# First mixer of a two-block network: parameters in two transfers, x in eight, the norm's sums by token on TensorE, and fewer small VectorE operations

## The reference

```
h = rmsnorm(x, even_norm)                  # over 1024 features of each token
p = h @ even_w_in                          # 2048 columns: u (512), z (1024), pool (512)
u -> state-space layer (32 groups of 16 channels, complex decay exp(dt * (a_re + i a_im)),
     dt = exp(log_dt)), evaluated in chunks of 8 tokens: a Toeplitz part inside
     a chunk and a scan over 64 chunks
pool -> four causal running means (windows 2, 4, 8, 16), minus the input, times pool_w and pool_scale
out = (concat(pool, glu(s5)) * silu(z)) @ even_w_out ; x = x + out
```

## Time and profile before

| what | us |
|---|---|
| median of 3 runs | 2919.9 (2909.63 to 2922.06) |
| the profiled execution, its own time | 2919.66 |
| its span, first to last instruction | 2917.9 |
| TensorE busy in the span | 2700.2 (93%) |
| VectorE busy | 1556.8 (53%) |
| ScalarE busy | 948.7 (33%) |
| GpSimd busy | 351.6 (12%) |

### The profile page before, as it was taken

One profiled execution on the slowest core, in us unless ns is written; L12 is line 12 of the kernel. 1 busy time (PEld: TensorE's weight loads), 2 busy tenths in 40 slices (PEclk: granted clock), 3 DMA queues, 4 the chain that ended last, 5 costly groups with the idle time before them and its releaser, 6 DMA issues.

```text
span 2917.9 us, 31891 instructions
## 1 busy us (share of the span) xinstructions
PE 2700.2 (93%) x13104; PEld 2103.4 (72%) x13104; DVE 1556.8 (53%) x2110; ACT 948.7 (33%) x1536; POOL 351.6 (12%) x303
## 2 busy tenths in 40 slices
PE   4889997899999988799999999999999977999997
PEld 3667665678888766486788888888878634788885
DVE  8975897654433478645533334433365457443332
ACT  2214321532222442552323223222232435332321
POOL 1001000122210000010222102221000000122200
PEclk9889999899999998799999999999999879999998
DMA  3252211122232221001322332232323200132232
GB/s 113 78 92 94 89 44 50 66 88 101 94 101 91 79 69 58 22 2 37 102 99 96 96 100 94 94 101 90 98 90 107 67 15 1 58 101 95 98 100 69
DMA packets 75810, 229.02 MB, mean 78 GB/s; under 512 B 16656, under 2 KB 17936, under 8 KB 75280
## 3 DMA queue, kind: packets, MB, share of 16 engines
q1 hardware_dynamic: 62880, 213.51, 22.2%
q0 software_dynamic: 1840, 5.77, 1.0%
q10 hardware_dynamic: 10944, 7.70, 0.9%
HBM read 221.18 MB, written 5.77 MB: 78 GB/s over the span
## 4 chain that ended last, share of the span: by engine, by line
PE 72%; DVE 19%; ACT 4%; issue 2%; DMA 1%; ACTq 1%; POOL 0%; DVEq 0%; SPq 0%; POOLq 0%
PE ps L353 71%; DVE mem L370 6%; DVE mem L383 5%; DVE part L440 3%; ACT part L428 1%; PE ps L364 1%; DMA mem<-lag_dram 1%; DVE mem L548 1%; DVE mem L2793 1%; DVE ps L370 1%; ACT mem L504 1%; DMA mem<-in_w_even 1%; ACTq L1100 1%; DVE mem L376 0%; DVE mem L388 0%
## 5 line engine op out<-in xcount | busy, mean ns | idle before, releaser
L353 PE MATMUL ps<-part,part 128*128 128x512 f32 (+1 forms) x9624 | 2212.8, 391 | 71.4 <-DVE part L523 27.3
L353 PEld LDWEIGHTS ps<-part,part 128*128 128x128 f32 x9624 | 1799.4, 190 | 482.8 <-issue 45.7
L440 DVE TENSOR_TENSOR part<-mem,part 128x1024 fp32r<-128x1024 f32 (+2 forms) x421 | 560.1, 1337 | 588.3 <-ACT part L428 587.8
L428 ACT ACTIVATE part<-mem 128x1024 fp32r<-128x1024 f32 (+2 forms) x421 | 418.5, 1003 | 234.9 <-DMA mem<-in_ffb_down 56.4
L370 DVE TENSOR_TENSOR mem<-ps,mem 128x512 f32<-128x512 f32 (+3 forms) x356 | 221.8, 623 | 351.1 <-PE ps L353 336.6
L353 PE MATMUL ps<-mem 128*64 128x64 f32 (+14 forms) x2728 | 341.6, 333 | 60.5 <-DVE mem L370 29.6
L353 PEld LDWEIGHTS ps<-mem 128*64 128x64 f32 (+4 forms) x2728 | 214.8, 170 | 173.8 <-issue 88.8
L512 POOL TENSOR_TENSOR mem<-mem 128x512 f32<-128x512 f32 x70 | 92.5, 1321 | 1378.7 <-ACT mem L504 1376.9
L370 DVE TENSOR_TENSOR mem<-mem 128x512 f32<-128x512 f32 (+13 forms) x335 | 169.7, 506 | 41.5 <-ACT mem L1490 11.4
L1463 ACT ACTIVATE part<-mem 128x512 fp32r<-128x512 f32 x88 | 55.6, 632 | 328.6 <-DVE mem L370 328.6
L1472 POOL TENSOR_TENSOR mem<-mem 128x512 f32<-128x512 f32 x88 | 113.9, 1294 | 378.8 <-ACT mem L1460 378.8
(11 more groups left out here) (160 smaller groups left out, 907.5 us busy)
## 6 DMA issues: line engine op xcount, KB each, us to landing
mem<-in_ffa_gate SPq DMA_DIRECT2D x44, 512.0 KB, 3.2
mem<-in_ffa_up SPq DMA_DIRECT2D x44, 512.0 KB, 3.2
mem<-in_ffb_gate SPq DMA_DIRECT2D x44, 512.0 KB, 3.2
mem<-in_ffb_up SPq DMA_DIRECT2D x44, 512.0 KB, 3.2
mem<-in_ffa_down SPq DMA_DIRECT2D x32, 512.0 KB, 3.5
mem<-in_ffb_down SPq DMA_DIRECT2D x32, 512.0 KB, 3.6
mem<-in_w_odd SPq DMA_DIRECT2D x24, 512.0 KB, 3.2
mem<-in_w_ab SPq DMA_DIRECT2D x22, 512.0 KB, 3.2
```

The lines of the kernel that those rows point to most:

```text
L353: return e.matmul(out, l, r, start=start, stop=stop, skip_group_check=True)
L428: w.e.activation(K.wts[c % NH].h[:, 0:n], K.raws[c % NR][:, 0:n], ACT.Copy).then_inc(*K_A.up(("w", c)))
L440: w.e.tensor_tensor(t.l, K.raws[c % NR][:, 0:n], t.hf, SUB).then_inc(*K.V.up(("w", c)))
```

## The change

The columns that VectorE needs first (`even_norm`, `log_dt`, `a_re`, `a_im`, 104 of the 816) come by a transfer of their own, `params0`. The other 712 are issued later by ScalarE, behind its last square, and `ssm_bc` behind them. SP issues weight chunk 0 first, then x in eight transfers of one tile. VectorE and ScalarE start with `params0` alone. GpSimd no longer adds the squares: TensorE multiplies each 128x128 piece of each square tile by a column of ones, so that the sums of a token come out with tokens as rows (128x4 in place of 128x512), and the scale, reciprocal and root run on 128x4. To get the factor back along the row, VectorE multiplies the identity by the four columns (`spread`, 128x512), TensorE multiplies that by ones, and ScalarE copies the result out of PSUM into `rstd`. `exp_small` has 15 operations in place of 22, `even_u_vector` one of 512 columns in place of eight of 64 (the chunk is now reversed when it is read back from DRAM), and the pool takes its mean and difference in one operation.

The diff, without the lists of semaphore names and of host arrays:

```diff
@@ -26,7 +26,7 @@
 
 
 COLS = [
-    ("even_norm", 8), ("pool_scale", 4), ("ssm_d", 8), ("log_dt", 32), ("a_re", 32), ("a_im", 32),
+    ("even_norm", 8), ("log_dt", 32), ("a_re", 32), ("a_im", 32), ("pool_scale", 4), ("ssm_d", 8),
     ("odd_norm", 8), ("conv_w", 248), ("conv_b", 8), ("ln_g", 8), ("ln_b", 8), ("final_norm", 8),
     ("ffa_norm", 16), ("mix_norm", 16), ("ffb_norm", 16), ("mu", 14), ("w0", 4), ("a0", 4),
     ("kk", 4), ("ka", 4), ("rk", 4), ("lnw", 4), ("lnb", 4), ("subln", 1), ("mconv_w", 16),
@@ -37,6 +37,7 @@
 for _name, _n in COLS:
     COL[_name] = NCOL
     NCOL += _n
+FIRST = COL["pool_scale"]
 
 
 CONSTS = [
@@ -675,6 +676,7 @@
         self.ys = bc.rearrange("p (q i c) -> p q i c", q=4, i=LC)
         high = m.tiles(5)
         self.y = [late[:, 2048 + T * i:2048 + T * i + T] for i in range(3)] + [high[:, i, :] for i in range(5)]
+        self.root, self.spread = K.rT, K.nb[2]
         self.lags = K.nb01.rearrange("p (a n) -> p a n", a=8)
 
     def part(self, a, tl):
@@ -691,9 +693,18 @@
     E, e = K.even, w.e
     K.ring(0, 1, 2, 3, 4, 5, 6, 7)
     h_ready = lambda k: (K.V, ("h", 0, k))
+    sums = K.take(w, ("msT", 0), K.V)
+    for k in range(8):
+        w.wait_ge(*K.A["sq", 0, k])
+        for t in range(NT):
+            done = mm(e, sums[:, t:t + 1], K.sq[k % 2][:, t * P:(t + 1) * P], K.cc("ones", 0, 1), k == 0 and t == 0,
+                      k == 7)
+        done.then_inc(*K.P.up(("summed", k), *([("msT", 0)] if k == 7 else [])))
     for o in linear(K, w, "even_u", 4, 8, K.h, h_ready, K.V):
         if o == 0:
-            norm_tensor(K, w, 0, K.ss)
+            acc = K.take(w, "even_factor", K.A)
+            w.wait_ge(*K.V["even_spread"])
+            mm(e, acc, K.cc("ones"), E.spread, True, True).then_inc(*K.P.up("even_factor"))
     zed = linear(K, w, "even_z", 8, 8, K.h, h_ready, K.V)
     pool = linear(K, w, "even_pool", 4, 8, K.h, h_ready, K.V)
     next(zed)
@@ -771,19 +782,17 @@
 def exp_small(w, E, out, in_, *names):
 
     t0, t1, t2 = E.v[6:9]
-    ts(w, t0, in_, 1.0 / math.log(2.0), None, MUL, None)
-    ts(w, t0, t0, -126.0, 126.0, MAX, MIN)
-    ts(w, t0, t0, 12582912.0, None, ADD, None)
+    ts(w, t0, in_, 1.0 / math.log(2.0), -126.0, MUL, MAX)
+    ts(w, t0, t0, 126.0, 12582912.0, MIN, ADD)
     ts(w, t0, t0, -12582912.0, None, ADD, None)
     stt(w, t1, t0, -0.693359375, in_, MUL, ADD)
     stt(w, t1, t0, 2.12194440e-4, t1, MUL, ADD)
     ts(w, t1, t1, -0.7, 0.7, MAX, MIN)
-    ts(w, t2, t1, 1.0 / 5040, 1.0 / 720, MUL, ADD)
-    for c in (1.0 / 120, 1.0 / 24, 1.0 / 6, 0.5, 1.0, 1.0):
-        tt(w, t2, t2, t1, MUL)
-        ts(w, t2, t2, c, None, ADD, None)
+    ts(w, t2, t1, 1.0 / 5040, None, MUL, None)
+    for c in (1.0 / 720, 1.0 / 120, 1.0 / 24, 1.0 / 6, 0.5, 1.0):
+        stt(w, t2, t2, c, t1, ADD, MUL)
     ts(w, E.v[12].bitcast(I32), t0, 127.0, 8388608.0, ADD, MUL)
-    tt(w, out, t2, E.v[12], MUL, *names)
+    stt(w, out, t2, 1.0, E.v[12], ADD, MUL, *names)
 
 
 def even_angles(K, w):
@@ -927,8 +936,7 @@
     E = K.even
     w.wait_ge(*K.P["even_u", o])
     acc, factor = positions(K.acc("even_u", o)), positions(K.rstd)
-    for d in range(LC):
-        tt(w, E.us[:, o, 64 * d:64 * d + 64], acc[:, 7 - d, :], factor[:, 7 - d, :], MUL, ("even_u", o))
+    tt(w, E.us[:, o, :].rearrange("p (j c) -> p j c", j=LC), acc, factor, MUL, ("even_u", o))
 
 
 def even_z_vector(K, w, o):
@@ -957,8 +965,8 @@
         sh *= 2
     oth = a[0] if cur is not a[0] else a[1]
     tt(w, oth[:, 0:16], cur[:, 0:16], K.cc("invpos", 16 * o, 16), MUL)
-    ts(w, oth[:, 16:T], cur[:, 16:T], 1.0 / width, None, MUL, None)
-    tt(w, E.pooled[o % 2], oth, u, SUB, ("pooled", o))
+    stt(w, E.pooled[o % 2][:, 16:T], cur[:, 16:T], 1.0 / width, u[:, 16:T], MUL, SUB)
+    tt(w, E.pooled[o % 2][:, 0:16], oth[:, 0:16], u[:, 0:16], SUB, ("pooled", o))
     weights_lo(K, w, K.first[0] + 12 + o + 4)
 
 
@@ -968,13 +976,19 @@
     even_angles(K, w)
     weights_lo(K, w, c + 1)
     for k in range(8):
-        w.wait_ge(*K.landed(f"x{k // 2}"))
+        w.wait_ge(*K.landed(f"x{k}"))
         gained_vector(K, w, 0, k, lambda k: K.pc("even_norm", k))
+    weights_lo(K, w, c + 2)
+    w.wait_ge(*K.landed("consts"))
+    w.wait_ge(*K.landed("params"))
+    rstd_vector(K, w, ("msT", 0), E.root, K.acc("msT", 0)[:, 0:4], 1.0 / 1024, 1e-6)
     weights_lo(K, w, c + 3)
+    w.wait_ge(*K.A["rstd", ("msT", 0)])
+    tt(w, E.spread.rearrange("p (t n) -> p t n", t=NT), b(K.cc("ident"), [P, NT, P], 1), b(E.root, [P, NT, P], 2), MUL,
+       "even_spread")
     even_factors(K, w)
-    rstd_vector(K, w, ("ms", 0), K.rstd, K.acc("ms", 0), 1.0 / 1024, 1e-6)
     even_powers(K, w)
-    w.wait_ge(*K.A["rstd", ("ms", 0)])
+    w.wait_ge(*K.A["even_factor"])
     even_u_vector(K, w, 0)
     weights_lo(K, w, c + 4)
     even_u_vector(K, w, 1)
@@ -1050,19 +1064,25 @@
 def even_scalar(K, w):
     E, e = K.even, w.e
     c = K.first[0]
-    e.dma_start(E.bc, K.io["ssm_bc"]).then_inc(*K.counts["ssm_bc"].up("landed", by=16))
     weights_hi(K, w, c + 1)
     for k in range(8):
-        w.wait_ge(*K.landed(f"x{k // 2}"))
+        w.wait_ge(*K.landed(f"x{k}"))
         gained_scalar(K, w, 0, k, lambda k: K.pc("even_norm", k))
-        square_scalar(K, w, 0, k, K.ss, K.sq)
+        if k > 1:
+            w.wait_ge(*K.P["summed", k - 2])
+        e.activation(K.sq[k % 2], K.x[:, k, :], ACT.Square).then_inc(*K.A.up(("sq", 0, k)))
+    e.dma_start(K.prm[:, FIRST:NCOL], K.io["params"]).then_inc(*K.counts["params"].up("landed", by=16))
+    e.dma_start(E.bc, K.io["ssm_bc"]).then_inc(*K.counts["ssm_bc"].up("landed", by=16))
+    weights_hi(K, w, c + 2)
+    rstd_scalar(K, w, ("msT", 0), E.root)
     weights_hi(K, w, c + 3)
     w.wait_ge(*K.V["angle"])
     e.activation(E.turn, E.angle, ACT.Abs).then_inc(*K.A.up("turn"))
     e.activation(E.si, E.angle, ACT.Sin).then_inc(*K.A.up("sine"))
+    w.wait_ge(*K.P["even_factor"])
+    e.activation(K.rstd, K.acc("even_factor"), ACT.Copy).then_inc(*K.A.up("even_factor"))
     w.wait_ge(*K.V["quarter"])
     e.activation(E.co, E.turn, ACT.Sin).then_inc(*K.A.up("cosine"))
-    rstd_scalar(K, w, ("ms", 0), K.rstd)
     for o in range(4):
         weights_hi(K, w, c + o + 4)
     for o in range(8):
@@ -1078,7 +1098,7 @@
                 w.wait_ge(*K.landed(f"u_out{tl}"))
                 for d in range(LC):
                     e.dma_start(E.u[16 * d:16 * d + 16, 8 * tl:8 * tl + 8, :],
-                                K.u_dram[tl].rearrange("(g h) d c -> d h g c", h=16)[d]).then_inc(
+                                K.u_dram[tl].rearrange("(g h) j c -> j h g c", h=16)[7 - d]).then_inc(
                         *K.counts[f"u_in{tl}"].up("landed", by=16))
         if o == 4:
             for i in range(2):
@@ -1130,9 +1150,7 @@
 def even_gpsimd(K, w):
     E, e = K.even, w.e
     c = K.first[0]
-    for k in range(8):
-        square_gpsimd(K, w, 0, k, K.ss, K.sq)
-    w.wait_ge(*K.P["ms", 0])
+    w.wait_ge(*K.P["even_factor"])
     zeros = K.nb[2]
     memset(w, zeros, 0.0)
     w.wait_ge(*K.G.now)
@@ -3027,9 +3045,6 @@
 def sync(K, e):
 
     w = Waits(e, K.P)
-    for i in range(4):
-        e.dma_start(K.x[:, 2 * i:2 * i + 2, :], K.io["x"][:, 2 * i:2 * i + 2, :]).then_inc(
-            *K.counts[f"x{i}"].up("landed", by=16))
     for c, (src, n, _) in enumerate(K.weights):
         if c >= NR:
             w.wait_ge(*K.lo_count(c - NR)["w", c - NR])
@@ -3037,6 +3052,9 @@
         if len(src.shape) == 3:
             dst = dst.rearrange("p (a b) -> p a b", a=src.shape[1])
         e.dma_start(dst, src).then_inc(*K.counts[f"raw{c % NR}"].up(c, by=16))
+        if c == 0:
+            for k in range(8):
+                e.dma_start(K.x[:, k, :], K.io["x"][:, k, :]).then_inc(*K.counts[f"x{k}"].up("landed", by=16))
     w.wait_ge(*K.V["final", 9, 7])
     e.dma_start(K.io["out"], K.x).then_inc(*K.counts["out"].up("landed", by=16))
     w.wait_ge(*K.landed("out"))
@@ -3045,7 +3063,6 @@
 def tensor(K, e):
     w = Waits(e, K.P)
     w.wait_ge(*K.landed("consts"))
-    w.wait_ge(*K.landed("params"))
     even_tensor(K, w)
     odd_tensor(K, w)
     swiglu_tensor(K, w, 3)
@@ -3060,8 +3077,7 @@
 
 def vector(K, e):
     w = Waits(e, K.V)
-    w.wait_ge(*K.landed("consts"))
-    w.wait_ge(*K.landed("params"))
+    w.wait_ge(*K.landed("params0"))
     even_vector(K, w)
     odd_vector(K, w)
     swiglu_vector(K, w, 3, 4, lambda k: K.pc("mix_norm", k))
@@ -3076,9 +3092,9 @@
 
 def scalar(K, e):
     w = Waits(e, K.A)
-    e.dma_start(K.prm[:, :], K.io["params"]).then_inc(*K.counts["params"].up("landed", by=16))
+    e.dma_start(K.prm[:, 0:FIRST], K.io["params0"]).then_inc(*K.counts["params0"].up("landed", by=16))
     e.dma_start(K.cst[:, 0:LATE], K.io["consts"]).then_inc(*K.counts["consts"].up("landed", by=16))
-    w.wait_ge(*K.landed("params"))
+    w.wait_ge(*K.landed("params0"))
     even_scalar(K, w)
     odd_scalar(K, w)
     swiglu_scalar(K, w, 3, 4, lambda k: K.pc("mix_norm", k))
```

4 lines of the change are left out of this document (2 added, 2 removed).

## The result

The changed kernel takes 2907.4 us, the median of 9 runs (2900.58 to 2912.97). Nine runs of the kernel before on the same chip gave 2923.1 us (2909.63 to 2928.26). The ratio is 0.9946, 95% interval 0.9932 to 0.996, which is 15.7 us less, 11.7 to 19.9 by the interval. The profiled execution took 2907.43 us, 12.2 less than the profiled one of before. The forecast was 2901.7, with its own range 2897 to 2906 and a wide one 2893 to 2911; the measured median lies in the wide one alone. C came at 96.48 us instead of 108.3: 11.8 us earlier, where 18.0 were forecast.

The account below looks back on a forecast made before the run. Two equally long ways (to 1.4 us) leave the opening at C, TensorE's queue and VectorE with transfers, so only C's earlier arrival counts. Gains less losses on VectorE's path sum to 18.0 us: 2919.7 to 2901.7, own range 2897 to 2906, wide 2893 to 2911.

Parts of the forecast that it names:

- 1 start: Opening: `params0` lands at 4.5 us, so VectorE starts there instead of at 8.11; 3.6 us won (1.9 to 5.3).
- 2 `exp_small`: VectorE's small operations in the opening: two calls lose seven operations each, at 0.22 us; 3.0 us won.
- 3 GpSimd gone: VectorE without GpSimd adding squares beside it: small operations win 3.7 us, the eight L523 win 2.2 us.
- 4 norm, spread: VectorE's scale and reciprocal on 128x4 win 3.7 us; the 128x512 spread costs 0.7.
- 5 chunk 2: New VectorE wait behind the reciprocal, for ScalarE's root and weight chunk 2's high part; 1.3 us lost.
- 6 cosine: Cosine behind TensorE's spread product and ScalarE's copy, ready at 27.2 us; VectorE waits 2.1 instead of 0.3, 1.8 lost.
- 7 u tiles: VectorE's four u tiles, one operation of 1.0 us each instead of eight taking 2.40; 5.6 us won (5.4 to 6.8).
- Rival A: u tile 0 runs at TensorE's lower clock, making the cosine 3.0 us later; time 2904.7, chance 0.2.
- Rival B: Behind C, another lower-clock stretch of TensorE costs 5 to 7 us: 2908, chance 0.17; the opposite, 2895, chance 0.12.
- Rivals C and D: TensorE at 1.2 GHz from C to first state output, 2950, chance 0.03; something else paces VectorE, 2910, chance 0.06.
- Term 8: `ssm_bc` and late parameters issued 10 us later (16.5), weight chunks and pool: no effect; late parameters have some 2 us in hand.
- rival D: The gain does not reach C because something else, such as weight chunks landing, paces VectorE; 2910, chance 0.06.

## Why the prediction was right, and where its size failed

By the time: right in direction and in the wide range of 2893 to 2911, 5.7 us above the number and 1.4 above the forecast's own range of 2897 to 2906. The base was 3.4 us low (2919.7, where nine runs gave 2923.1), so of the 18.0 us forecast the median gained 15.7. By C, where the terms were counted, it is 11.8 of 18.0; that the median came nearer to its forecast than C did is luck, as far as the runs show. Term by term:

| term | forecast | measured | from |
|---|---|---|---|
| 1 start | 3.6 | 3.3 | first operation 8.11 to 4.78 |
| 2 `exp_small` | 3.0 | 3.0 | 12.95 - 8.11 = 4.84 to 8.11 - 4.78 = 3.33, twice |
| 3 GpSimd gone | 5.9 | 6.9 | 10.19 to the rest of chunk 0, less 3.33 and 3.0, is 3.9; L524 8.43 to 5.38, 3.05 |
| 4 norm, spread | 3.0 | 3.0 | 4.15 to 0.38, and 0.80 to the next start |
| 5 chunk 2 | -1.3 | -1.2 | the bracket at 23.80 |
| chunk 1 and the sums | 0 | -1.6 | the brackets 1.21 and 0.40 |
| 6 cosine | -1.8 | -4.9 | 5.21 for 0.30 |
| 7 u tiles | 5.6 | 5.1 | 1.07 to 1.16 each, where 2.35 to 2.42 stood |
| z tile 2 | 0 | -1.8 | 3.58 for 1.76 |

These make 11.8.

**The step that failed** is in term 6, "TensorE's four products a tile took 0.95 us elsewhere and keep up". That row was read behind other work, at the upper clock. Here TensorE had nothing ahead of the sums, ran them at the lower clock at 1.72 us a tile, and held back ScalarE, whose squares I had at 1.13. The last square ended 3.3 us late (19.26 for 16). From it follow: chunk 1's high part late for VectorE (1.21), the sums late (0.40), u tile 0 starting at 21.87 instead of 16.7, and the cosine, queued behind the spread product and the copy, ready at 31.2 instead of 27.2. Two runs show the cause: where the clock was up, after ten dummy products or after the first wide sums, ScalarE didn't wait; and in the run with the dummy products the waits came back when it fell. At the lower clock both forms are longer than a square's 1.13 us (1.72 for four one-column products, 2.05 for the first wide one), so the form matters through the clock that it gets. The size of the cosine's loss then came from the queue: with the cosine first it is 0.30 us and C 4.9 to 5.4 us earlier, z tile 2's wait left out.

**The sum of waits isn't a sum of costs.** Term 3 measured 6.9 us, but giving GpSimd its work back costs only 2.0 at C; the two waits of 1.2 us are worth 0.2. As soon as VectorE waits for the chain of squares, sums, u tile 0, copy and cosine, what it does ahead of that wait is hidden. I had written that a shift of the start is "partly swallowed" there, and didn't carry that over to terms 2, 3 and 5.

**Rival A** gave the cosine 3.0 us more, a time of 2904.7, and "5 would be rival A" as its mark. The mark appeared, 5.21, but the mechanism was another: u tile 0 took 7.74 us, less than the 8.46 of before, which the forecast had in its sum. Its first 4 us did run at the lower clock (11 records, then 19 in as long a time), but not all of it. The clock had been low one step earlier too, in the sums, and that was not in the forecast. The same number would have followed from both, and only the starts (21.87) tell them apart.

**Rival B** (given back behind C): not in the first pair of profiles, 11.8 at C and 12.2 at the end. It did happen in the second profile of the changed kernel: 14.3 ahead of the first profile of before at C, 10.2 near 300 us, and 1.8 at the end (8.5 against the second profile of before). That execution, 2917.91 us, was the longest of eight, three of which took 2915 to 2918 where the others took 2904 to 2908. Stretches at the lower clock move in both directions, and by the 5 to 7 us that B had or more: +4.0 and +6.7 in the second profile of before, and from -24.4 to -14.3 near 210 us between two profiles of one kernel. So B describes single executions, not the median. This is also the plainest reading of why the median gained 15.7 while C gained 11.8 to 14.3: the profiled execution of before, 2919.66, was itself below the 2921.66 to 2925.86 that its medians came to in four comparisons. The interval, 11.7 to 19.9, allows the gain at C alone; more isn't shown.

**Rivals C and D** didn't happen. The stretch from C to the first state output took 60 us, as before, with the 4.26 us of idle time ahead of the lags unchanged, and the wait for the Toeplitz blocks is 0.99 where it was 1.42, so both ways out of the opening are still equally long. **Term 8** held for `ssm_bc` and the pool. The late parameters, issued at 18.64 instead of 16.5 us, landed 3.2 us later, some 0.4 us ahead of the norm's scale and not 2. And rival D's argument that VectorE's one wait ahead of C keeps its distance failed: z tile 2's 24 products may fall into a stretch at the lower clock, which cost 1.8 us against before and 2.7 against the changed kernel's second profile.

A version that beats both kernels at C is the changed one with the cosine ahead of the copy: 88.68 against 94.00 and 108.3, with a median of 2901.88 and a ratio to before of 0.9933 (0.9917 to 0.9949). Against the changed kernel itself the intervals overlap.

## What to carry to other kernels

Read a duration only together with what its engine did before: a TensorE row from the middle of a kernel is no price for an opening, where one-column products ran at half speed and paced another engine through its two buffers. Where an engine's queue holds a short result that others wait for (a cosine of 0.22 us) behind a long chain, put it first; here that one exchange was worth 5 us at C. And add terms only along one chain: once a wait for another engine remains, what was saved ahead of it is hidden, and the next thing late is that engine's.

## What the runs showed of the hardware that was not expected

- 32 one-column products in a row, with TensorE shown as busy throughout, left its clock low, and it fell from 2.4 to 1.2 GHz during them when ten wider products had lifted it. Four of them by themselves took 1.84 us at the lower level (the run with GpSimd's additions) and 0.95 at the upper, so they are slowed by nearly the ratio of the clocks despite their single column.
- Where stretches at the lower clock fall differs between executions of the same kernel. It moved C by 2.5 us (96.48 and 94.00), and the time behind C by up to 9 us with C equal (108.3 and 108.27).
- Eight operations of L524 that don't wait for each other took 5.38 us, 0.67 each, though each is 0.74 long: they overlap. I had added a gap instead.
- `params0`, 52 KB, took 4.0 us to land beside weight chunk 0, where 32 KB later in the program took 2.0. The 2.1 us that stands beside term 1 as an estimate was too short by 1.9.
